# Where the normalised rows wait, and how far the expert weights run ahead, in a two-block kernel on one core

## The chip, the core and the metric

One core of a Trainium2 chip runs the whole program: TensorE (PE, with its weight loads listed as PEld), VectorE (DVE), ScalarE (ACT), GpSimd (POOL) and SyncE (SP), which here only issues DMAs. The metric is the device time of one execution in microseconds. Three runs of the kernel before took 2300.44, 2300.65 and 2302.3 us; the median is 2300.65 us.

## The reference

The program computes two transformer-like blocks on 512 tokens of 1024 channels in float32. The change lies in the last part of the second block, the mixture of experts, and in the last normalisation:

```python
def _rmsnorm(x, g):
    inv = lax.rsqrt(jnp.mean(xf * xf, axis=-1, keepdims=True) + RMS_EPS)
    return xf * inv * g

def _hier_moe(h, wg, bg, we, be, w_gate, w_up, w_down):      # 512 tokens, 64 experts of 1024 x 512
    g_prob = softmax(ht @ wg + bg);  p_g, g_idx = top_k(g_prob, 1)
    e_sel = (ht @ we + be)[group g_idx];  top_l, top_i = top_k(e_sel, 2)
    gate_w = p_g * softmax(top_l);  expert = g_idx * 8 + top_i
    # for every expert, on the rows that chose it:
    a = silu(xb @ w_gate[e]) * (xb @ w_up[e]);  y = a @ w_down[e]
    # each token: sum over its two experts of gate_w * y

x = x + merged @ w_out
hn = _rmsnorm(x, ffn_norm_g)
x = x + _hier_moe(hn, ...)
return _rmsnorm(x, final_norm_g)
```

## The kernel before

All tokens stay in `X` (128 partitions, 4 row blocks i of 1024 columns). The program is written out by hand for each engine, and semaphores alone order the engines among each other. What matters here are three stretches.

**Router.** For each block i, PE multiplies by the output matrix (`project`, L1034), VectorE adds into `X`, ScalarE squares, and the normalising factor `block_r` comes out. PE turns the rows (`turn`, L1045) and makes the router's products (`logits`, L1055). VectorE chooses the experts (`choose`), PE makes a running count of rows of each expert (`rank`, L1071), and VectorE makes from it the table of which token stands in which slot (`place`, `pair_of`). ScalarE writes the normalised rows `Z[:, i, :] = block_r * X` in a turned column order (L1652) and stores them to `hn_d` (L1655), from which the rows of every later pair of experts are gathered. The first pair's rows are not gathered: `first_rows` (L1090) makes them with 64 PE instructions, `Z` as the stationary operand times a selection matrix `OG`. `Z` lies in the first 4096 columns of the work zone.

**Expert pairs.** 64 experts are taken as 32 pairs q, each with room for 64 rows of each expert. A pair needs six matrices of 2 MB: gate, gate, up, up, down, down, numbered n = 6q to 6q+5 (`in_eg`, `in_eu`, `in_ed` in the rows). SyncE loads them in that order (L2920) into a ring of ten slots, `RING`; the slot of matrix n is free again when PE has finished matrix n-10. In the ring's first turn the slots still hold earlier work, so n = 0 waits for the gated products, n = 6 and 7 wait for the output products, n = 8 for the last of these, and n = 9, whose slot is the zone of `Z`, for `hn` 64 (all four blocks stored) and for the first pair's rows. Matrices 10 to 13 are loaded in quarters behind the gate and up products of pair 0 (`refill_first`, L3029); from n = 14 on whole matrices are loaded. PE's pair is: rows turned (L1175), gate and up (L1193, 64 instructions), turn (L1204), down (L1230, 32 instructions). Pairs of odd q are spread onto the tokens by products (`pe_spread`, L1164), the others are stored and gathered. Behind pair 0 PE makes the table of weights (L1139) and the count of rows (`cnt`, L1143), from which the number of further rounds follows.

**End.** Pair 31's down matrices come in three parts (`last0`, `last1`, `last2`), the products (L1218) follow them, eight spread products L1164 and additions L2624 put them onto `X`, ScalarE loads the table of the square root (L1689), squares eight half blocks (L1692), VectorE makes the factor, scales each block (L2710), and SyncE stores it (L3079).

Of the kernel before, what the change touches and what calls it, by code (L numbers as in the profile page):

```python
# [15 lines left out]
CAP = 64  # L16
# [6 lines left out]
SBUF = 55940  # L23
RING = (6, 2, 0, 4, 8, 9, 3, 1, 5, 7)
# [4 lines left out]
def _cols(table, spec):  # L29
    at = 0  # L30
    for name, n in spec:
# [9 lines left out]
CK_N = _cols(CK_COLS, [("ident", 128), ("iota", 128), ("tok", 8), ("gf", 8), ("gx", 8), ("neg", 128), ("cneg", 124), ("c01", 124),  # L41
                       ("tri", 128), ("ones", 128), ("cs", 256)])
# [116 lines left out]
def program(nc, A, out):  # L159
    with ExitStack() as ctx:  # L160
# [202 lines left out]
        done_ck = SB[:, 4096 + CK_COLS["neg"][0]:4096 + CK_N + SM_N + 8 * 72 + 72 + 400]  # L363
# [62 lines left out]
        def tensor_program(pe):  # L426
# [697 lines left out]
            rank(3)  # L1124
            first_rows(2, 1)
# [6 lines left out]

            for q in range(PAIRS):
                pe_pair(pe, T, q, lambda n: loaded("ex", 6 * q + n), lambda n: slot("ex", 6 * q + n), any_bank, ("gather", q % 2, 16 * ((q + 1) // 2)))
                if q == 0:
                    o = open_tile(pe, ("wtab",), any_bank())
                    pe.wait_ge(S("bw"), 1)
                    for n in range(8):
                        ins = pe.matmul(o[:, 0:PAIRS], AM[:, n // 4, n % 4, :], BW[:, n, :], start=n == 0, stop=n == 7)  # L1139
                    ins.then_inc(T.f("wtab"), 1)  # L1140
                    o = open_tile(pe, ("cnt",), any_bank())
                    for j in range(4):
                        ins = pe.matmul(o[:, 0:64], ck("ones"), ES[:, j, :], start=j == 0, stop=j == 3)  # L1143
                    ins.then_inc(T.f("cnt"), 1)
                for n in range(6):
                    W.ended[("ex", 6 * q + n)] = (("g", q), ("g", q), ("u", q), ("u", q), ("d", q, 1), ("d", q, 1))[n]
            pe_spread(pe, PAIRS - 1, LAST_TILES[2:], any_bank)
# [18 lines left out]
        def pe_pair(pe, table, q, ready, weight, bank, gathered):  # L1166
# [12 lines left out]
            for mat, name in enumerate(("g", "u")):  # L1179
# [5 lines left out]
                for k in range(8):  # L1185
# [6 lines left out]
                    for e in range(2):  # L1192
                        ins = pe.matmul(o[64 * e:64 * e + 64, :], x[:, k, 64 * e:64 * e + 64],  # L1193
                                        weight(2 * mat + e)[:, 512 * k:512 * k + 512], start=k == 0, stop=k == 7)
# [14 lines left out]
            if q == PAIRS - 1:  # L1209
                both = [open_tile(pe, ("d", q, nh), bank(), 1, table) for nh in range(2)]  # L1210
                for nh, ks, part in ((0, range(4), 0), (1, range(2), 1), (1, range(2, 4), 2)):
                    if part == 2:
                        pe_spread(pe, q, LAST_TILES[0:2], bank)
                    pe.wait_ge(S(f"last{part}"), 32)
                    for k in ks:
                        for e in range(2):
                            d = 1024 * k + 512 * nh
                            ins = pe.matmul(both[nh][64 * e:64 * e + 64, :], aT[:, k, 64 * e:64 * e + 64], weight(4 + e)[:, d:d + 512],  # L1218
# [6 lines left out]
            for nh in range(2):  # L1225
                o = open_tile(pe, ("d", q, nh), bank(), 1, table)
                for k in range(4):
                    for e in range(2):
                        d = 1024 * k + 512 * nh
                        ins = pe.matmul(o[64 * e:64 * e + 64, :], aT[:, k, 64 * e:64 * e + 64], weight(4 + e)[:, d:d + 512],  # L1230
# [7 lines left out]
        LAST_TILES = [(i, nh) for nh in range(2) for i in range(4)]  # L1238
        BEHIND_X = [(0,), (1,), (2,), (3,), (8,), (9,), (10, 11), (12, 13)]
# [8 lines left out]
        def scalar_program(act):  # L1248
# [388 lines left out]
            for i in range(4):  # L1637
# [17 lines left out]
                act.dma_start(hn_d[128 * i:128 * i + 128, :], Z[:, i, :]).then_inc(S("hn"), 16)  # L1655
# [8 lines left out]
        def act_pair(act, table, q):  # L1664
# [9 lines left out]
            for nh in range(2) if q == PAIRS - 1 else (1,):  # L1674
                act.wait_ge(*table.full("d", q, nh))
# [6 lines left out]
        def results_taken(eng, table, q):  # L1682
            if q - 1 in STORED:
                eng.wait_ge(S("y_st"), 16 * (STORED.index(q - 1) + 1))
            elif q and table is T:
                eng.wait_ge(*table.full("sp", q - 1, 3, 1))

        def act_end(act):
            act.activation(s5, s5, ACT.Sqrt, scale=0.0)  # L1689
            for i, nh in LAST_TILES:  # L1690
                act.wait_ge(S("xadd"), LAST_TILES.index((i, nh)) + 1)
                act.activation(Z[:, i, 512 * nh:512 * nh + 512], X[:, i, 512 * nh:512 * nh + 512], ACT.Square,  # L1692
                               accum_out=h5[:, i, nh:nh + 1]).then_inc(S("l_sq"), 1)
# [6 lines left out]
        def vector_program(dve):  # L1700
# [829 lines left out]
            def place(i):  # L2530
# [6 lines left out]
                for c in range(2):  # L2537
                    t = tt(OC[:, c, :], AM[:, c, i, :], bc(BM0[:, c, i], 1, 128), ALU.mult)
# [20 lines left out]

            def weights():  # L2560
                for i in range(4):
# [21 lines left out]
            def count_rounds():  # L2583
                dve.wait_ge(*T.full("cnt"))
                dve.tensor_reduce(cnt, T.ap("cnt")[:, 0:64], op=ALU.max, axis=AX.X).then_inc(T.s("cnt"), 1)
                dve.wait_ge(*T.free("cnt"))
                after(ts(cnt, cnt, float(CAP - 1), None, ALU.add))
                after(own(dve.tensor_copy(NR, cnt)))
                dve.tensor_scalar(NR, NR, CAP.bit_length() - 1, None, ALU.logical_shift_right).then_inc(S("rounds"), 1)

            for q in range(ENDS):
                dve_pair(dve, T, q, weights if q == 0 else None)
                if q == 0:
                    copy(("wtab",), WTAB, T.ap("wtab")[:, 0:PAIRS])
                    count_rounds()
# [110 lines left out]
        def dve_end(dve):  # L2706
            dve_last(dve, Count(S("last")))
            dve.wait_ge(S("row2"), 16)
            for i in range(4):
                dve.scalar_tensor_tensor(Z[:, i, :], X[:, i, :], r5[:, i:i + 1], row2, ALU.mult, ALU.mult).then_inc(S("fin_row"), 1)  # L2710
# [199 lines left out]
        def sync_program(sp):  # L2910
# [109 lines left out]
            def refill_first(n):  # L3020
                mat = (n - len(RING)) // 2
                for part in range(4):
# [5 lines left out]
                    for e in range(2):  # L3028
                        sp.dma_start(slot("ex", n + e)[:, cols], EW[(n + e) % 6 // 2][2 * ((n + e) // 6) + (n + e) % 2][:, cols]).then_inc(  # L3029
                            loaded("ex", n + e)[0], 16)  # L3030

            for n in range(6 * PAIRS):
# [43 lines left out]
        def sync_end(sp):  # L3076
            for i in range(4):
                sp.wait_ge(S("fin_row"), i + 1)
# [246 lines left out]
```

## Time and profile before

| | us |
|---|---|
| median of three runs | 2300.65 |
| the profiled execution, its own time | 2298.54 |
| its span | 2296.7 |
| PE busy | 2176.2 |
| DVE busy | 936.3 |
| ACT busy | 349.3 |

The page's second part cuts the span into 40 slices of 57 us and shows in each how busy each engine and the 16 DMA engines were. PE is nearly always busy by that view, but its busy share holds for stretches with different limits, so the chain of waits and the rows by stretch say which of PE and the DMA engines sets the pace. The DMA engines moved 563.57 MB, 530.70 MB of it on the queue of SyncE and ScalarE.

### The profile page before, as it was taken

To read this page: it belongs to the slowest core of one execution; us is meant where nothing else is said; L and a number is where in the kernel's file an instruction comes from. 1 tells how busy PE (TensorE), PEld (TensorE's weight loads), DVE (VectorE), ACT (ScalarE), POOL (GpSimd) and SP (SyncE) were. 2 spreads that over 40 slices of the span, in tenths; PEclk is the share of its full clock that TensorE was granted. 3 is DMA by queue.
4 is the path that set the end of the run, shared out by engine and by line. 5 is a ranking of instruction groups with operands and counts; after the bars stand their busy time and mean duration, and the time that the engine had idled before them with its cause. 6 is when DMAs were issued, how large, how long until landed. Compare 5 with 4: busy or idle time off the path is not lost.

```text
span 2296.7 us, 23080 instructions
## 1 busy us (share of the span) xinstructions
PE 2176.2 (95%) x9050; PEld 1131.4 (49%) x9050; DVE 936.3 (41%) x1815; ACT 349.3 (15%) x678; POOL 297.2 (13%) x260
## 2 busy tenths in 40 slices
PE   9999999999999999999999999999999899888886
PEld 6544444475887644477588553333333333333332
DVE  2256544542876587537544342222222222222224
ACT  2015324201222200021101210000000000000001
POOL 0001121221376100001053010000000000000001
PEclk9999999999999999999999999999999999999999
DMA  7211110330333444483332499999999999999997
GB/s 291 101 56 47 55 46 10 115 151 10 110 131 132 160 183 183 172 149 116 128 138 110 201 345 425 427 426 426 426 427 427 426 427 426 426 427 427 427 427 278
DMA packets 75709, 563.57 MB, mean 245 GB/s; under 512 B 21202, under 2 KB 25938, under 8 KB 43152
## 3 DMA queue, kind: packets, MB, share of 16 engines
q1 hardware_dynamic: 52544, 530.70, 57.7%
q10 hardware_dynamic: 15136, 22.71, 3.0%
q0 software_dynamic: 7920, 8.67, 1.1%
q8 instruction: 74, 1.21, 0.2%
q14 instruction: 35, 0.29, 0.0%
HBM read 558.59 MB, written 27.82 MB: 255 GB/s over the span
## 4 chain that ended last, share of the span: by engine, by line
PE 69%; DMA 21%; DVE 6%; SPq 1%; issue 1%; ACT 1%; POOL 0%; DVEq 0%; ACTq 0%; POOLq 0%
DMA sb<-in_eu 13%; PE ps L1193 9%; PE ps L522 9%; PE ps L850 8%; DMA sb<-in_ed 8%; PE ps L429 7%; PE ps L1230 6%; PE ps L771 5%; PE ps L1006 5%; PE ps L454 3%; PE ps L1034 2%; PE ps L732 2%; DVE sb L1704 2%; PE ps L710 2%; PE ps L1164 2%; SPq L3064 1%
## 5 line engine op out<-in xcount | busy, mean ns | idle before, releaser
L1193 PE MATMUL ps<-sb 128*64 128x512 f32 x2048 | 463.0, 607 | 50.9 <-DMA sb<-in_eu 42.4
L1193 PEld LDWEIGHTS ps<-sb 128*64 128x64 f32 x2048 | 163.8, 139 | 337.1 <-issue 337.1
L1704 DVE TENSOR_TENSOR sb<-sb 128x1024 f32<-128x1024 f32 (+9 forms) x419 | 226.4, 573 | 86.3 <-PE ps L850 38.3
L522 PE MATMUL ps<-sb 128*128 128x512 f32 x512 | 236.7, 600 | 0.0
L1230 PE MATMUL ps<-sb 128*64 128x512 f32 x992 | 221.4, 599 | 14.0 <-ACT sb L1672 8.3
L850 PE MATMUL ps<-sb 128*128 128x512 f32 x448 | 193.4, 593 | 1.4 <-DVE sb L2255 1.4
L429 PE MATMUL ps<-sb 128*128 128x512 f32 (+1 forms) x464 | 188.9, 566 | 1.0 <-issue 1.0
L771 PE MATMUL ps<-sb 128*128 128x256 f32 x784 | 175.7, 383 | 3.6 <-DVE sb L2175 3.6
L771 PEld LDWEIGHTS ps<-sb 128*128 128x128 f32 x784 | 148.5, 191 | 25.3 <-DVE sb L2175 4.0
L1230 PEld LDWEIGHTS ps<-sb 128*64 128x64 f32 x992 | 70.6, 137 | 151.9 <-issue 134.9
L522 PEld LDWEIGHTS ps<-sb 128*128 128x128 f32 x512 | 91.0, 190 | 100.3 <-issue 98.6
L850 PEld LDWEIGHTS ps<-sb 128*128 128x128 f32 x448 | 84.6, 190 | 106.7 <-issue 106.7
L429 PEld LDWEIGHTS ps<-sb 128*128 128x128 f32 x464 | 87.6, 190 | 96.1 <-issue 92.7
L1164 PE MATMUL ps<-sb 128*128 128x512 f32 x256 | 119.6, 599 | 0.0
L2696 DVE SCALAR_TENSOR_TENSOR sb<-sb,ps 128x512 f32<-128x512 f32 x32 | 22.1, 690 | 238.3 <-PE ps L1193 238.3
L2691 DVE SCALAR_TENSOR_TENSOR sb<-sb,ps 128x512 f32<-128x512 f32 x32 | 22.1, 690 | 222.5 <-ACT sb L1668 222.5
L1006 PE MATMUL ps<-sb 128*128 128x256 f32 x504 | 109.2, 379 | 1.0 <-issue 1.0
L1006 PEld LDWEIGHTS ps<-sb 128*128 128x128 f32 x504 | 95.7, 190 | 14.7 <-issue 1.8
L1262 ACT ACTIVATE sb<-ps 128x512 f32<-128x512 f32 (+3 forms) x98 | 51.6, 536 | 319.5 <-PE ps L429 54.3
L2624 DVE TENSOR_TENSOR sb<-sb,ps 128x512 f32<-128x512 f32 x128 | 88.0, 688 | 29.8 <-PE ps L1164 29.8
L2742 POOL TENSOR_TENSOR sb<-sb 128x256 f32<-128x256 f32 (+3 forms) x32 | 41.7, 1302 | 351.7 <-DVE sb L1921 351.6
L2686 DVE TENSOR_TENSOR sb<-ps,sb 128x512 f32<-128x512 f32 x64 | 41.4, 688 | 101.3 <-PE ps L1175 100.7
(347 smaller groups left out, 2055.5 us busy)
## 6 DMA issues: line engine op xcount, KB each, us to landing
sb<-in_eu SPq DMA_DIRECT2D x63, 2048.0 KB, 36.7
sb<-in_eg SPq DMA_DIRECT2D x62, 2048.0 KB, 37.3
sb<-in_ed SPq DMA_DIRECT2D x60, 2048.0 KB, 37.3
sb<-in_m SPq DMA_DIRECT2D x16, 2048.0 KB, 7.4
sb<-in_m SPq DMA_DIRECT2D x16, 1024.0 KB, 4.9
sb<-in_mg SPq DMA_DIRECT2D x8, 1536.0 KB, 6.5
sb<-in_wo SPq DMA_DIRECT2D x4, 2048.0 KB, 7.7
sb<-in_winF SPq DMA_DIRECT2D x12, 512.0 KB, 3.5
```

The source lines that it names most:

```text
L429: ins = pe.matmul(out, lhsT, rhs, start=k == 0, stop=k == len(pieces) - 1)
L454: ins = pe.matmul(T.ap(*tile)[:, t], lhsT, rhs[:, t], start=k == 0, stop=k == 7)
L522: ins = pe.matmul(o, lhsT, rhs, start=k == 0, stop=k == 7)
L771: ins = pe.matmul(T.ap(*name)[:, 256 * (f % 2):256 * (f % 2) + 256], a[:, j], b[:, j], start=j == 0, stop=j == 3)
L850: ins = pe.matmul(T.ap("m2", turn, f), a[j], b[j], start=s_ == 0 and j == 0, stop=s_ == 7 and j == 1)
L1006: ins = pe.matmul(o[:, 256 * f:256 * f + 256], a[:, j], b[:, j], start=j == 0, stop=j == n - 1)
L1164: pe.matmul(o, OH[o_ % 2][:, i, :], YE[:, 512 * nh:512 * nh + 512], start=True, stop=True).then_inc(T.f("sp", q, i, nh), 1)
L1193: ins = pe.matmul(o[64 * e:64 * e + 64, :], x[:, k, 64 * e:64 * e + 64], weight(2 * mat + e)[:, 512 * k:512 * k + 512], start=k == 0, stop ...
L1230: ins = pe.matmul(o[64 * e:64 * e + 64, :], aT[:, k, 64 * e:64 * e + 64], weight(4 + e)[:, d:d + 512], start=k == 0, stop=k == 3)
L1262: act.activation(dst, T.ap(*name) if src is None else src, ACT.Copy).then_inc(T.s(*name), 1)
L1704: return own(dve.tensor_tensor(o, a, b, op))
L2624: dve.tensor_tensor(xs, xs, T.ap("sp", q, i, nh), ALU.add).then_inc(S("xadd") if q == PAIRS - 1 else T.s("sp", q, i, nh), 1)
```

## The change

1. **Columns.** In the table of constants, `neg`, `cneg` and `cs` now stand last and 40 columns are added. The constants of finished work give two regions: `HELD`, 1024 columns, for the normalised rows of blocks 0 to 2 one after the other (block 3 takes `YE`), and `FIRST_HALF`, 2048 columns, for half a matrix.
2. **Rows.** ScalarE writes each block's normalised rows to `HELD[i]` and, from block 1 on, first waits until the block before is stored. `first_rows` reads `X` itself, in the order `(a b) -> b a`: its 128 stationary columns now lie 8 floats apart. The factor `block_r` goes into the selection matrix.
3. **Ring.** The zone of `Z` becomes the slot of matrix 6, which waits for the last gated product alone; 7, 8 and 9 take the slots that were those of 6, 7 and 8. The first half of matrix 10 is loaded into `FIRST_HALF` once block 2 is stored and the products `rank` 3 and `cnt` are done.
4. **Count.** The product `cnt` moves from behind pair 0 to behind `rank` 3, its reduction to the start of VectorE's `weights`.
5. **End.** Two spread products go ahead of the product of `last1` and two ahead of that of `last2` (before: two ahead of `last2`). A square root whose result nobody reads stands ahead of ScalarE's copy in pair 31. Block 3 is scaled and stored in two halves.

```diff
-RING = (6, 2, 0, 4, 8, 9, 3, 1, 5, 7)
+RING = (6, 2, 0, 4, 8, 9, 7, 3, 1, 5)
+AHEAD = len(RING)
+        HELD = [view(done_ck, at_ck, 1024)] * 3 + [YE]
+        FIRST_HALF = view(done_ck, 0, 2048)
             def first_rows(i, hf):
-                pe.wait_ge(S("hn_rows"), i + 1)
                 pe.wait_ge(S("first"), i + 1)
-                zr = Z[:, i, :].rearrange("p (b a) -> p b a", b=8)
+                zr = X[:, i, :].rearrange("p (a b) -> p b a", b=8)
...
             rank(3)
+            open_tile(pe, ("cnt",), 4)
+            for j in range(4):
+                ins = pe.matmul(T.ap("cnt")[:, 0:64], ck("ones"), ES[:, j, :], start=j == 0, stop=j == 3)
...
+            def expert(n, at_):
+                return (FIRST_HALF if n == AHEAD and at_ < 2048 else slot("ex", n))[:, at_:at_ + 512]
...
-                    if part == 2:
-                        pe_spread(pe, q, LAST_TILES[0:2], bank)
+                    if part:
+                        pe_spread(pe, q, LAST_TILES[2 * part - 2:2 * part], bank)
...
-                act.activation(Z[:, i, :].rearrange("p (b a) -> p b a", b=8), X[:, i, :].rearrange("p (a b) -> p b a", b=8),
+                if i:
+                    act.wait_ge(S("hn"), 16 * i)
+                act.activation(HELD[i].rearrange("p (b a) -> p b a", b=8), X[:, i, :].rearrange("p (a b) -> p b a", b=8),
                                ACT.Copy, scale=block_r[:, i:i + 1]).then_inc(S("hn_rows"), 1)
...
+                if q == PAIRS - 1 and nh == 0:
+                    act.activation(s5, r5, ACT.Sqrt, scale=0.0)
...
-                    t = tt(OC[:, c, :], AM[:, c, i, :], bc(BM0[:, c, i], 1, 128), ALU.mult)
+                    t = own(dve.scalar_tensor_tensor(OC[:, c, :], AM[:, c, i, :], block_r[:, i:i + 1], bc(BM0[:, c, i], 1, 128),
+                                                     ALU.mult, ALU.mult))
...
+                if n == 6:
+                    sp.wait_ge(*T.full("mgp", 3, 3, 3))
-                if n == 8:
+                if n == 9:
                     sp.wait_ge(*T.full("wo2", 3, 1))
-                if n == 9:
-                    sp.wait_ge(S("hn"), 64)
-                    sp.wait_ge(*T.full("xt", 0, 1))
+                if n == AHEAD:
+                    sp.wait_ge(S("hn"), 48)
+                    sp.wait_ge(*T.full("rank", 3))
+                    sp.wait_ge(*T.full("cnt"))
+                    for part in range(2):
+                        cols = slice(1024 * part, 1024 * part + 1024)
+                        sp.dma_start(FIRST_HALF[:, cols], EW[k // 2][2 * q + k % 2][:, cols]).then_inc(loaded("ex", n)[0], 16)
```

PE's order from the turns of block 3 on, before (a row is a line, an operation and how many in a run; a product counts once here and as two instructions in the trace; L1090 is `first_rows`, L1143 `cnt`, L1193 pair 0's gate and up, L1175 the turns of pair 1):

```order
L1090 MATMUL ps<-sb 128x128 x12
L1071 MATMUL ps<-sb 128x64
L1090 MATMUL ps<-sb 128x128 x4
L1078 MATMUL ps<-sb 128x32 x2
L1090 MATMUL ps<-sb 128x128 x8
L1078 MATMUL ps<-sb 128x32 x2
L1193 MATMUL ps<-sb 64x512 x32
L1204 MATMUL ps<-sb 128x128 x4
L1230 MATMUL ps<-sb 64x512 x16
L1139 MATMUL ps<-sb 128x32 x8
L1143 MATMUL ps<-sb 128x64 x4
L1175 MATMUL ps<-sb 128x128 x8
```

The same place after the change (`first_rows` is L1093, `rank` L1075, `cnt` L1130, gate and up L1199):

```order
L1093 MATMUL ps<-sb 128x128 x12
L1075 MATMUL ps<-sb 128x64
L1130 MATMUL ps<-sb 128x64 x4
L1093 MATMUL ps<-sb 128x128 x4
L1082 MATMUL ps<-sb 128x32 x2
L1093 MATMUL ps<-sb 128x128 x8
L1082 MATMUL ps<-sb 128x32 x2
L1199 MATMUL ps<-sb 64x512 x32
L1210 MATMUL ps<-sb 128x128 x4
L1236 MATMUL ps<-sb 64x512 x16
L1149 MATMUL ps<-sb 128x32 x8
L1181 MATMUL ps<-sb 128x128 x8
```

The four products of the count have left the place between pair 0 and pair 1 and stand ahead of pair 0.

ScalarE's order from its copy in pair 31 to the end, after the change (L1685 is the added square root, L1707 the one of before, L1690 the copies of pair 31's results; the branches are those of the loop of further rounds):

```order
L1681 ACTIVATE sb<-ps 128x512
L1685 ACT_TABLE_LOAD
L1685 ACTIVATE sb<-sb 128x4
L1690 ACTIVATE sb<-ps,sb 128x512 x2
L3170 TENSOR_LOAD sb
...
L3173 UNCONDITIONAL_BRANCH
L1707 ACT_TABLE_LOAD
L1707 ACTIVATE sb<-sb 128x4
L1703 ACTIVATE sb<-sb 128x512 x8
L1711 ACTIVATE sb<-sb 128x4
```

A table load has been added at L1685; the one ahead of the squares still stands, at L1707.

## Rows read from the trace of the kernel before

**Rows 1.** Page, part 2: DMA, tenths of 40 slices.
```profile
DMA  7211110330333444483332499999999999999997
```

**Rows 2.** Chain of waits: start us, us, what.
```profile
1793.80 42.03 DMA sb<-in_eu
```

**Rows 3.** Stretches: length, busy PE, PEld, DVE, ACT, POOL; clock, DMA share, GB/s.
```profile
1300.00:1310.00 10.00, 10.00 (x41) 5.71 (x40) 5.42 (x26) 4.05 (x6) 0.00 (x0) 1.00 0.13 52
...
1344.00:1346.00 2.00, 2.00 (x12) 0.65 (x10) 1.69 (x10) 0.33 (x2) 0.00 (x0) 1.00 0.34 133
...
1480.00:2200.00 720.00, 651.43 (x2818) 248.28 (x2814) 156.99 (x266) 44.90 (x73) 38.22 (x38) 0.98 1.01 426
```

**Rows 4.** Order of time, SyncE's issues: start us, us, what.
```profile
1321.44 0.33 SPq L2920 DMA_DIRECT2D sb<-in_eg  x1
...
1331.79 0.43 SPq L2920 DMA_DIRECT2D sb<-in_eu  x1
...
1346.05 0.33 SPq L2920 DMA_DIRECT2D sb<-in_eu  x1
```

**Rows 5.** Landing (last number) of issues at 1331.42, 1331.79, 1346.05, 1366.31, 1378.00.
```profile
sb<-in_eg SPq DMA_DIRECT2D x1, 2048.0 KB, 7.8
...
sb<-in_eu SPq DMA_DIRECT2D x1, 2048.0 KB, 13.8
...
sb<-in_eu SPq DMA_DIRECT2D x1, 2048.0 KB, 8.2
...
sb<-in_eu SPq DMA_DIRECT2D x1, 2048.0 KB, 15.5
...
sb<-in_ed SPq DMA_DIRECT2D x1, 2048.0 KB, 13.6
```

**Rows 6.** DMA issues of 1372 to 1600, median us to landing.
```profile
sb<-in_ed SPq DMA_DIRECT2D x18, 2048.0 KB, 25.9
```

**Rows 7.** Order of time, PE in the router's end and behind pair 0.
```profile
1335.29 2.90 PE L1090 MATMUL ps<-sb 128*128 128x128 f32 x24
...
1340.55 2.02 PE L1090 MATMUL ps<-sb 128*128 128x128 f32 x16 [0.87 <-DVE sb L2540]
...
1342.87 13.96 PE L1193 MATMUL ps<-sb 128*64 128x512 f32 x64
...
1368.01 1.08 PE L1143 MATMUL ps<-sb 128*128 128x64 f32 x8
```

**Rows 8.** Order of time: weight loads and copies, columns side by side or apart.
```profile
1332.17 0.42 PEld L1045 LDWEIGHTS ps<-sb 128*128 128x128 f32 x4
...
1385.75 0.56 PEld L1204 LDWEIGHTS ps<-sb 128*128 128x128 f32 x4 [1.79 <-issue]
...
1243.83 1.06 ACT L1625 ACTIVATE sb<-sb 128x1024 f32<-128x1024 f32 x1 [9.58 <-DVE sb L1978]
...
1284.86 2.15 ACT L1652 ACTIVATE sb<-sb 128x1024 f32<-128x1024 f32 x1 [1.00 <-DVE sb L2494]
```

**Rows 9.** Order of time, VectorE ahead of pair 1's gate product.
```profile
1370.04 1.29 DVE L2686 TENSOR_TENSOR sb<-ps,sb 128x512 f32<-128x512 f32 x2
```

**Rows 10.** Order of time, the end.
```profile
2271.70 0.69 ACT L1679 ACTIVATE sb<-ps,sb 128x512 f32<-128x512 f32 x1 [5.03 <-PE ps L1218]
...
2273.55 1.94 PE L1218 MATMUL ps<-sb 128*64 128x512 f32 x8 [1.88 <-DMA sb<-in_ed]
...
2275.41 1.99 PE L1164 MATMUL ps<-sb 128*128 128x512 f32 x4
...
2277.33 1.94 PE L1218 MATMUL ps<-sb 128*64 128x512 f32 x8
...
2280.40 1.28 ACT L1689 ACT_TABLE_LOAD   x1 [0.40 <-issue]
```

**Rows 11.** Chain of waits, the squares.
```profile
2281.90 4.92 ACT sb L1692 x16
```

**Rows 12.** Stretches, while blocks are stored.
```profile
2292.00:2293.00 1.00, 0.00 (x0) 0.00 (x0) 1.00 (x2) 0.00 (x0) 0.00 (x0) 0.50 1.00 401
```

More of the change, by code:

```diff
@@ L22 @@
 GELU = math.sqrt(2.0 / math.pi)
-SBUF = 55940
-RING = (6, 2, 0, 4, 8, 9, 3, 1, 5, 7)
+SBUF = 55980
+RING = (6, 2, 0, 4, 8, 9, 7, 3, 1, 5)
+AHEAD = len(RING)
 SM_COLS = {}
@@ L1140, in tensor_program @@
                     ins.then_inc(T.f("wtab"), 1)
[L1141 to L1144, printed above, removed]
                 for n in range(6):
                     W.ended[("ex", 6 * q + n)] = (("g", q), ("g", q), ("u", q), ("u", q), ("d", q, 1), ("d", q, 1))[n]
-            pe_spread(pe, PAIRS - 1, LAST_TILES[2:], any_bank)
+            pe_spread(pe, PAIRS - 1, LAST_TILES[4:], any_bank)
             pe.wait_ge(S("rounds"), 1)
@@ L1193, in pe_pair @@
                         ins = pe.matmul(o[64 * e:64 * e + 64, :], x[:, k, 64 * e:64 * e + 64],
-                                        weight(2 * mat + e)[:, 512 * k:512 * k + 512], start=k == 0, stop=k == 7)
+                                        weight(2 * mat + e, 512 * k), start=k == 0, stop=k == 7)
                     if table is T and q == 0 and k in (1, 3, 5):
@@ L1238, in program @@
         LAST_TILES = [(i, nh) for nh in range(2) for i in range(4)]
+        LAST_ROWS = [(i, slice(0, 1024)) for i in range(3)] + [(3, slice(512 * nh, 512 * nh + 512)) for nh in range(2)]
         BEHIND_X = [(0,), (1,), (2,), (3,), (8,), (9,), (10, 11), (12, 13)]
@@ L2557, in vector_program, with count_rounds @@
             dve_table(dve, own, T)
+            def count_rounds():
+                dve.wait_ge(*T.full("cnt"))
+                dve.tensor_reduce(cnt, T.ap("cnt")[:, 0:64], op=ALU.max, axis=AX.X).then_inc(T.s("cnt"), 1)
+                dve.wait_ge(*T.free("cnt"))
+                after(ts(cnt, cnt, float(CAP - 1), None, ALU.add))
+                after(own(dve.tensor_copy(NR, cnt)))
+                dve.tensor_scalar(NR, NR, CAP.bit_length() - 1, None, ALU.logical_shift_right).then_inc(S("rounds"), 1)
             def weights():
+                count_rounds()
                 for i in range(4):
@@ L2580, in weights @@
                 dve_rows(dve, own, ENDS, EVEN)
[L2583 to L2589, printed above, removed]
             for q in range(ENDS):
@@ L2708, in dve_end @@
             dve.wait_ge(S("row2"), 16)
-            for i in range(4):
-                dve.scalar_tensor_tensor(Z[:, i, :], X[:, i, :], r5[:, i:i + 1], row2, ALU.mult, ALU.mult).then_inc(S("fin_row"), 1)
+            for i, cols in LAST_ROWS:
+                dve.scalar_tensor_tensor(Z[:, i, cols], X[:, i, cols], r5[:, i:i + 1], row2[:, cols], ALU.mult, ALU.mult).then_inc(S("fin_row"), 1)
         def dve_last(dve, own):
@@ L3028, in refill_first @@
                     for e in range(2):
+                        if n + e == AHEAD and part < 2:
+                            continue
                         sp.dma_start(slot("ex", n + e)[:, cols], EW[(n + e) % 6 // 2][2 * ((n + e) // 6) + (n + e) % 2][:, cols]).then_inc(
@@ L3076, in sync_end @@
         def sync_end(sp):
-            for i in range(4):
-                sp.wait_ge(S("fin_row"), i + 1)
-                sp.dma_start(out[128 * i:128 * i + 128, :], Z[:, i, :]).then_inc(S("fin"), 16)
-            sp.wait_ge(S("fin"), 64)
+            for n, (i, cols) in enumerate(LAST_ROWS):
+                sp.wait_ge(S("fin_row"), n + 1)
+                sp.dma_start(out[128 * i:128 * i + 128, cols], Z[:, i, cols]).then_inc(S("fin"), 16)
+            sp.wait_ge(S("fin"), 80)
         R_more, R_pair = (Psum(PS, T.s_full, T.s_free) for _ in range(2))
```

29 lines of the change are left out of this document (17 added, 12 removed).

## The prediction

> **What bounds the kernel now.** I read the page's second part first, then the chain of waits, then the table of stretches and the landing times of SyncE's loads.
>
> The DMA row of the page is at 9 in every slice from about 1310 us on, and has holes only before [rows 1]. In the chain of waits of the late pairs the long pieces are transfers, such as 42.03 us of an up matrix [rows 2], and from 1480 to 2200 us the DMA share is 1.01 at 426 GB/s while PE is busy 651 of 720 us [rows 3]. So from pair 5 or so the end of the program is: the moment from which the DMA engines never rest, and the bytes still to be moved. Nothing in the change takes bytes away. It can help only by moving bytes into the holes, which are in the router's stretch: share 0.13 in 1300 to 1310 us, and 0.34 in 1344 to 1346 us [rows 3], and the last hole decides.
>
> How near the DMA engines are to a hole at any later time is told by the landings. A 2 MB load that finds the engines idle lands after 7.8 us (8.2 for another) [rows 5]. What a load takes over that is work queued ahead of it. Matrix 14, issued at 1366.31 when PE frees its slot, takes 15.5: 7.7 us are queued ahead. Matrix 16, issued at 1378.00 behind pair 1's gate product, takes 13.6: only 5.8 us. By 1372 to 1600 the median of the down matrices is 25.9 [rows 6]; PE gets through a pair faster there than the engines bring one, so the queue grows.
>
> **Part 1, the ring: what is gained before PE comes in.** Matrix 6 goes out behind matrix 5 at some 1266 us, into the hole. Of the old issues at 1321.44, 1331.79 and 1346.05 [rows 4] the last goes: matrix 9 now takes the place of matrix 8 and lands where that landed, 1331.79 + 13.8 = 1345.6, not at 1346.05 + 8.2 = 1354.2. That is 8.6 us of lead: one matrix (4.9 us at 426 GB/s) and the hole in which matrix 9 waited for the last rows to be stored. The half of matrix 10 (2.5 us), sent when the count is done at about 1339, keeps the engines busy until the first quarters are free, so the lead isn't lost at once.
>
> **Part 2: how much of the lead survives.** The following slots are freed by PE, and PE is no faster. Matrix 14 can't be led by more than the 7.7 us queued ahead of it, matrix 16 by no more than 5.8, plus what PE gains up to there. PE gains the count: four products (0.92 us until the turns can begin) from 1368.01 [rows 7], and VectorE's copy of the turned rows, which stood behind the count's reduction and began at 1370.04 [rows 9]. With the count away the first half of the rows is turned at about 1368.01 + 0.42 + 0.2 and copied from 1368.7: 1.35 us sooner. So the bound at matrix 16 is 5.8 + 1.35 = 7.15 us, the smallest of the three. Later ones have larger queues and the same 1.35 us. If PE's start of pair 0 slips by d, all these bounds shrink by d: the gain is 7.15 - d.
>
> **Part 3: d, what it costs PE.** The 64 instructions of `first_rows` stand in PE's row with no gap but one of 0.87 us [rows 7]: 24 take 2.90 us with the tail of the last, 0.112 us each. Their weight loads now read columns 8 floats apart. No row shows a weight load so. The nearest on PE are the turns at L1204, 4 floats apart: four loads in 0.56 us against 0.42 for columns side by side [rows 8], 0.035 us more each; the other near row is on ScalarE, where the copy of 1024 columns 8 floats apart takes 2.15 us and a tanh of 1024 side by side 1.06 [rows 8], a factor of 2.03. Bounds: nothing (the load is hidden under the product), 64 x 0.035 = 2.2 us by the first, 64 x 0.112 x 1.03 = 7.4 us by the second; beyond it a load could cost what ScalarE's element costs in time, 2.15/1024 x 128 = 0.27 us, 64 x 0.16 = 10 us. The product itself takes about as long as the load, so a doubled load has nothing to hide under. I take the factor of distance 8, a little rounded down for overlap: 6.5 us.
>
> The Trainium skill, SBUF — State Buffer, section "Door 1: The DMA port swizzle", says that the memory is read in lines of 16 bytes and that float32 may be read up to 4 elements apart for free, with a penalty beyond. The trace agrees as far as it goes: 4 apart costs PE little, 8 apart doubles ScalarE's time. The page gives no size; by it the free case is out, by the loads 4 apart alone it would be likely.
>
> The rest of the router: the count's four products (0.9 us) stand where PE waits 0.87 us for VectorE's L2540 [rows 7], so they cost nothing while the loads are cheap, and if the loads are dear that wait is gone and the count adds what the wait gave. The factor in the selection matrix replaces two operations of 128x128 by two of the same form: 0. The wait for `hn_rows` never ended last. ScalarE's new waits for its stores: each store has more than 9 us before the next copy needs it: 0. VectorE's reduction of the count (0.9 us) delays pair 0's gate step, which has the up product beside it (7 us of the 13.96 [rows 7]): 0. Pair 0 starts 6.5 us late, at 1349.4.
>
> Sum for the DMA stretch: -7.15 + 6.5 = -0.65 us.
>
> **Part 4, the end.** Before, PE's row is: `last1` lands, product at 2273.55, two spreads at 2275.41, `last2` lands, product at 2277.33 [rows 10]. ScalarE's copy, begun at 2271.70 and 0.69 long, lets spreads start at 2272.4. With two spreads there (1.8 us) the `last1` product starts at 2274.2, not 2273.55; then two more spreads, and the `last2` product at 2277.9, not 2277.33: +0.55. The spreads it takes forward don't matter, since the squares follow from ScalarE's last copy on: table load 1.28 us [rows 10], then eight squares back to back, 4.92 us [rows 11]. The order of instructions shows the table load of the end still in its place, and a second one added in pair 31 where ScalarE waits 5.03 us for a product [rows 10]: 0, no gain. Were the load gone, VectorE's additions would end last and 1.4 us would be had.
>
> The halved last block: while blocks are stored the DMA share is 1.00 at 401 GB/s [rows 12], so the stores follow the engines and not VectorE. A smaller last piece saves at most the 0.6 us that half a block takes to move; the extra operation costs 0.1. I take -0.1.
>
> **Sum.** -0.65 + 0.55 - 0.1 = -0.2 us against the profiled execution's 2298.54 (span 2296.7 and 1.84 around it). The runs' median is 2.1 us above that; against it the same difference gives 2300.4 us.
>
> **The rivals.** What can be told from no change here is about 0.2%, 4.6 us.
> - *The stride is hidden or nearly free on PE (d from 0 to 2).* For it: the loads 4 apart cost only 0.035 us, and loads are pulled ahead of products. Against: the factor 2 at distance 8 on ScalarE. Gain 5.2 to 7.15, end +0.45: 2294 to 2296, faster.
> - *Partly hidden (d from 2 to 5).* 2296 to 2299, within the band.
> - *The strided loads cost more than ScalarE's rate* (two readings of float32 per product both going line by line, and VectorE's chain waiting behind PE's `rank` 3, L1071). Place: the 64 loads before pair 0. It decides from d = 7.15 + 4.15 = 11.3 us, 0.29 us a load. At 0.33 us: d = 14, 2300.65 - 7.15 + 14 + 0.45 = 2308. For it only that no row shows distance 8 on PE. Slower.
> - *The lead isn't made*, because block 2's store lands late and holds the half matrix: then 1 us or so less in the free case, nothing in mine, where matrix 16 bounds.
>
> **Chances.** Forecast, load about doubled (d from 5 to 9, 2298.5 to 2302.5): 0.53. Free or nearly: 0.26. Partly hidden: 0.14. Dearer: 0.07. The range over all but two in ten, from the free case's lower end to a load somewhat above ScalarE's rate: 2293.8 to 2303.5. Faster by over 0.2% is the free case less its upper edge, 0.25; slower the dear one, 0.06; within, 0.69.
>
> **What would show it.** The group of weight loads of `first_rows`: near 0.21 to 0.23 us apart, and pair 0's first gate product near 1349. At 0.12 apart and 1343 the first rival holds. Matrix 9 should land at about 1345.6; matrix 16 should land 7.8 to 8 us after its issue, with a dip of the DMA share just before. The end from `last1` on should be half a microsecond longer, with a table load of 1.28 us still before the squares. I am wrong altogether if matrix 16's load takes much more than 8 us to land although the time doesn't fall, or if the DMA share has holes after 1400 us.

## The result, and the profile after

The changed kernel takes 2307.74 us (median of 9 runs, 2306.1 to 2309.61), the kernel before 2300.65 on the same chip: a ratio of 1.0031, 95% interval 1.0023 to 1.0040. It is slower, by 7.1 us, and lies outside the range. The profiled execution took 2306.10 us, 7.6 more than that of before, and its span is 7.3 us longer.

The page's DMA row reads like the one of before [rows 1]; averages over 58 us do not show what changed. The last row is the rate.

```profile
span 2304.0 us, 23083 instructions
...
DMA  7211110330333444483333589999999999999996
GB/s 290 100 55 47 55 46 10 113 152 10 110 131 132 164 178 182 183 152 116 113 137 114 237 308 422 425 425 426 426 425 426 426 425 426 426 426 426 426 426 267
```

PE in the router's end, in order of time (start, length, instructions). These are the lines of [rows 7]; L1093 is `first_rows`.

```profile
1333.16 1.94 PE L1093 MATMUL ps<-sb 128*128 128x128 f32 x8
...
1335.38 2.08 PE L1093 MATMUL ps<-sb 128*128 128x128 f32 x8
...
1339.02 5.97 PE L1093 MATMUL ps<-sb 128*128 128x128 f32 x24
1344.83 0.33 PE L1075 MATMUL ps<-sb 128*128 128x64 f32 x2
1345.00 1.06 PE L1130 MATMUL ps<-sb 128*128 128x64 f32 x8
1345.89 2.12 PE L1093 MATMUL ps<-sb 128*128 128x128 f32 x8
...
1348.21 4.08 PE L1093 MATMUL ps<-sb 128*128 128x128 f32 x16
1352.59 3.65 PE L1199 MATMUL ps<-sb 128*64 128x512 f32 x16
```

The 24 instructions that took 2.90 us take 5.97: 5.81/24 = 0.242 us each against 0.114. Over 64 that is 8.2 us; the difference of the five groups is 8.0. Pair 0's first gate product starts at 1352.59 instead of 1342.87 [rows 7], 9.7 us late. Of that 1.9 were lost before `first_rows`: this execution ran at half clock for 6.8 us from 92 us on, that of before for 3.4, which makes 1.7 of it. VectorE now waits for `rank` 3, which stands behind the 24 on PE:

```profile
1345.27 0.29 DVE L1720 TENSOR_TENSOR sb<-sb,ps 128x128 f32<-128x128 f32 x1 [3.60 <-PE ps L1075]
```

Behind pair 0, again PE:

```profile
1379.34 13.95 PE L1199 MATMUL ps<-sb 128*64 128x512 f32 x64 [0.54 <-DVE sb L2703]
...
1395.65 8.79 PE L1236 MATMUL ps<-sb 128*64 128x512 f32 x32 [0.69 <-ACT sb L1681]
```

Pair 1 starts 26.75 us after pair 0. Before it was 28.01 (1370.88 for its start), so the count's removal gave 1.3 us.

The DMA engines in the stretch where the last hole of before lay [rows 3]; the last two numbers are share and GB/s:

```profile
1345.00:1350.00 5.00, 5.00 (x30) 5.00 (x29) 2.79 (x11) 0.00 (x0) 0.00 (x0) 1.00 0.85 286
1350.00:1352.00 2.00, 2.00 (x10) 2.00 (x9) 0.69 (x1) 0.00 (x0) 0.00 (x0) 1.00 0.39 158
1352.00:1354.00 2.00, 2.00 (x14) 1.10 (x15) 1.53 (x8) 0.00 (x0) 0.00 (x0) 1.00 0.00 0
1354.00:1356.00 2.00, 2.00 (x12) 0.65 (x10) 1.76 (x14) 0.33 (x2) 1.40 (x2) 1.00 0.23 47
1356.00:1360.00 4.00, 4.00 (x22) 1.36 (x20) 3.38 (x17) 0.28 (x1) 0.81 (x1) 1.00 0.94 271
1360.00:1364.00 4.00, 4.00 (x22) 1.37 (x20) 0.69 (x1) 0.32 (x1) 0.00 (x0) 1.00 0.91 283
...
1480.00:2200.00 720.00, 652.65 (x2848) 251.52 (x2848) 159.53 (x269) 45.06 (x74) 38.56 (x38) 0.99 1.01 426
```

SyncE's issues, by which this reads: matrices 8 and 9 at 1333.36 and 1333.73 (landed at 1341.6 and 1347.9), the half matrix at 1346.14 (landed at 1352.05), the first quarter only at 1354.57, when pair 0 has used the first quarter of a slot, matrix 16 at 1386.46. So the engines stand idle for 2.5 us ahead of the first quarter. The quarters of matrices 10 to 13 are the first transfers that PE releases, and PE is late.

```profile
1333.36 0.80 SPq L2937 DMA_DIRECT2D sb<-in_eu  x2
1346.14 1.00 SPq L3069 DMA_DIRECT2D sb<-in_ed  x2
1354.57 6.29 SPq L3048 DMA_DIRECT2D sb<-in_ed  x6
...
1386.46 0.80 SPq L2937 DMA_DIRECT2D sb<-in_ed  x2
```

Landing of the matrix issued at 1386.46 (last number), against 13.6 in [rows 5]: nothing is queued ahead of it.

```profile
sb<-in_ed SPq DMA_DIRECT2D x1, 2048.0 KB, 8.8
```

Most of the lead is gone before matrix 16, though. Against before, this execution has moved 1.87 MB more by 1350 us, 1.04 MB less by 1364 and 1.65 less by 1400. Matrix 16 is issued 8.5 us later than before and lands 3.7 later (1395.3 against 1391.6); by matrix 24 the lag is 5.3, and the first half of the last up matrix lands at 2262.5 instead of 2257.2, 5.3 late. The rest arises at the end [rows 10]:

```profile
2274.33 1.28 ACT L1685 ACT_TABLE_LOAD   x1
2274.36 3.65 PE L1224 MATMUL ps<-sb 128*64 128x512 f32 x16 [0.69 <-ACT sb L1681]
...
2278.85 1.96 PE L1170 MATMUL ps<-sb 128*128 128x512 f32 x4 [0.83 <-issue]
2280.74 1.94 PE L1224 MATMUL ps<-sb 128*64 128x512 f32 x8
2282.61 1.98 PE L1170 MATMUL ps<-sb 128*128 128x512 f32 x4
2284.52 1.94 PE L1224 MATMUL ps<-sb 128*64 128x512 f32 x8
2286.51 0.69 ACT L1690 ACTIVATE sb<-ps,sb 128x512 f32<-128x512 f32 x1 [7.75 <-PE ps L1224]
...
2287.59 1.28 ACT L1707 ACT_TABLE_LOAD   x1 [0.39 <-issue]
```

The product of `last0` starts 6.35 us later than before (2274.36 against 2268.01), 1.05 more than the transfers' lag: PE's last pair waits for no transfer here, since the clock fell twice shortly before (share and clock at 2204 to 2212 below). From that product to ScalarE's last copy it is 12.15 us instead of 11.30, all of it work of PE but for 0.83 in which the first spread waits for ScalarE's copy: +0.85. From that copy to the end it is 17.5 us in both. 5.3 + 1.05 + 0.85 = 7.2.

The clock (the third number from the end, 0.5 is 1.2 GHz, 1 is 2.4) in three short stretches of the same execution:

```profile
94.00:98.00 4.00, 4.00 (x16) 2.07 (x13) 0.00 (x0) 0.00 (x0) 0.00 (x0) 0.50 0.05 16
...
1395.00:1400.00 5.00, 4.35 (x14) 1.35 (x16) 0.00 (x0) 0.59 (x1) 0.00 (x0) 0.66 1.01 429
...
2204.00:2212.00 8.00, 6.17 (x16) 2.09 (x18) 0.27 (x1) 0.00 (x0) 0.00 (x0) 0.57 1.00 418
```

Every profile here has such drops, 3.4 or 6.8 us long; each 3.4 us cost PE 1.7 (pair 1's 32 down products took 8.79 us at 1395.65, 7.09 at the full clock). Before these three PE had waited: 3.44 us, 0.94 and 0.69 around the turn L1210, and 2.92 us for an up matrix. The one at 1396 cost no transfer time, since the DMA engines were full (share 1.01).

### The profile page after: what moved, and what is told of

The parts are those of the page before. It is cut to its first block, busy times and chain, and to the rows that moved or that the text cites. A ratio compares the mean times of both kernels' runs of the same rounds, so it can differ in the third digit from the quotient of the medians.

```text
span 2304.0 us, 23083 instructions
## 1 busy us (share of the span) xinstructions
PE 2186.5 (95%) x9050; PEld 1140.8 (50%) x9050; DVE 936.8 (41%) x1816; ACT 350.6 (15%) x680; POOL 297.9 (13%) x260
## 4 chain that ended last, share of the span: by engine, by line
PE 72%; DMA 18%; DVE 7%; ACT 1%; issue 1%; ACTq 1%; SPq 0%; POOL 0%; DVEq 0%; POOLq 0%
DMA sb<-in_ed 12%; PE ps L1199 11%; PE ps L526 9%; PE ps L854 8%; PE ps L1236 7%; PE ps L433 6%; DMA sb<-in_eu 5%; PE ps L775 5%; PE ps L1010 5%; PE ps L1170 3%; PE ps L458 3%; PE ps L1038 2%; PE ps L736 2%; DVE sb L1720 2%; PE ps L714 2%
## 5 line engine op out<-in xcount | busy, mean ns | idle before, releaser
L1199 PE MATMUL ps<-sb 128*64 128x512 f32 x2048 | 458.4, 603 | 44.4 <-DMA sb<-in_eu 36.2
L1199 PEld LDWEIGHTS ps<-sb 128*64 128x64 f32 x2048 | 162.3, 139 | 327.5 <-issue 327.4
L1720 DVE TENSOR_TENSOR sb<-sb 128x1024 f32<-128x1024 f32 (+8 forms) x411 | 224.7, 579 | 86.1 <-PE ps L854 38.3
```

Source lines behind the costliest of these rows:

```text
L1720: return own(dve.tensor_tensor(o, a, b, op))
```

## The experiments

The runs come in three groups, named a_ and b_, p_, and c_, each on a chip of its own with its own runs of the kernel before (2300.22, 2300.41 and 2299.79 us, over 30 runs each). A median of about ten runs is good to some 2 us (the intervals), so differences of 1 us between two of them are weak alone. The same kernel under two names shows it: 2297.84 us as p_spread and 2296.26 as c_spread.

**The new ring with cheap loads (a_plain).** Pair 0's rows are read side by side from `X`, and the first four matrices are loaded with their rows in the same order; the factor of the norm follows.

```diff
-                zr = X[:, i, :].rearrange("p (a b) -> p b a", b=8)
+                zr = X[:, i, :].rearrange("p (b a) -> p b a", b=8)
...
-                                  bc(ck("gx")[:, 4 * hf:4 * hf + 4], 2, 128), ALU.mult).then_inc(table.s("xt", q, hf), 1)
+                                  bc(ck("gf" if table is T and q == 0 else "gx")[:, 4 * hf:4 * hf + 4], 2, 128), ALU.mult).then_inc(table.s("xt", q, hf), 1)
...
+                    if n < 4:
...
+                        sp.dma_start(shaped(slot("ex", n), 8, 512),
+                                     A[("eg", "eu")[k // 2]][k % 2].rearrange("(t p) n -> p t n", p=P)).then_inc(loaded("ex", n)[0], 16)
+                        continue
```

> The changed kernel, but the first pair's stationary columns of X lie side by side again: its gate and up matrices are loaded with row 128 t + p on partition p, so that the turned rows may be taken as contiguous blocks of 128. Nothing is left out of the computation. Theory 1 (the loads 8 apart cost PE about 8 us before pair 0, and PE frees the slots that bound the DMA engines): load spacing back from 0.24 to 0.11 us, pair 0's gate product 8 us sooner than in the changed kernel, the time 6 to 8 us below the changed kernel's and 0 to 1% of nothing else: about 2295 to 2300 where before gives 2300.65. Theory 2 (the loads cost little at the end, the loss is in the end or in the constants' new places): the time falls by less than 2 us against the changed kernel, to 2306 or more.

Measured 2296.74 us, ratio 0.9989 (0.9980 to 0.9998): within 2295 to 2300, and 11.0 us below the changed kernel (on another chip), more than the 6 to 8 expected. The loads are back at 0.114 us and pair 0 starts at 1343.29:

```profile
1335.66 2.90 PE L1093 MATMUL ps<-sb 128*128 128x128 f32 x24
...
1343.29 13.95 PE L1199 MATMUL ps<-sb 128*64 128x512 f32 x64
```

The rest of the change makes the kernel faster; the column order alone turns its sign. But the first half of the last up matrix lands at 2252.6, 4.6 us sooner than before, not 7. Matrix 9 and the half matrix do bring the lead: by 1350 us 2.92 MB more have moved than before (6.8 us at 426 GB/s). By 1360 it is 2.58, by 1390 2.20, by 1500 2.15 (5.0 us). The first part goes here:

```profile
1350.00:1352.00 2.00, 2.00 (x12) 0.65 (x10) 1.43 (x5) 0.60 (x1) 0.47 (x1) 1.00 0.94 262
1352.00:1354.00 2.00, 2.00 (x12) 0.64 (x10) 0.00 (x0) 0.00 (x0) 0.00 (x0) 1.00 0.93 258
```

The share is over 0.9 and the rate 260, against 408 and 363 in the same two stretches before: the queue is nearly empty and holds quarters and small stores and gathers. Matrix 14 lands 6.9 us sooner than before and matrix 16 only 5.45: it is issued 0.84 sooner (1377.16), and takes 9.0 us to land with nothing queued ahead of it, not 7.8.

A second part goes where the engines are full. From 1500 to 2200 us the two profiles with the old ring (before, b_apart) move 298.50 and 298.54 MB, the twelve with the new ring 297.94 to 298.06. These 0.5 MB are 1.1 us at the same DMA share of 1.01. The prediction has no term for them, and what in the new ring makes the rate lower stays open.

**The same with the end of before (a_plain_oldend), and the change with the end of before (a_oldend).** The edit on top of each:

```diff
-                if q == PAIRS - 1 and nh == 0:
-                    act.activation(s5, r5, ACT.Sqrt, scale=0.0)
...
-                    if part:
-                        pe_spread(pe, q, LAST_TILES[2 * part - 2:2 * part], bank)
+                    if part == 2:
+                        pe_spread(pe, q, LAST_TILES[0:2], bank)
...
-LAST_ROWS = [(i, slice(0, 1024)) for i in range(3)] + [(3, slice(512 * nh, 512 * nh + 512)) for nh in range(2)]
+LAST_ROWS = [(i, slice(0, 1024)) for i in range(4)]
```

> The same, with the end as before: spread products in the old order, no added square root, the last block scaled and stored whole. Theory 1 with my term for the end (0.45 us lost): 0.3 to 0.7 us below the run with the new end. Theory 2 (the end costs several us): 2 us or more below it.

> The changed kernel with the end as before. Theory 1: 2307.2, half a microsecond below the changed kernel, and the columns 8 apart keep the rest. Theory 2 (the end is the loss): 2304 or less.

Measured 2295.40 us, ratio 0.9981 (0.9972 to 0.9990), and 2305.28, ratio 1.0024 (1.0014 to 1.0034). The first is the best version found; it beats both kernels. It lies 1.3 us below a_plain and the second 2.5 below the changed kernel (another chip): each between what the two theories say, so the end costs more than 0.45 us. On one chip: the new end costs 1.3 us (2296.74 - 2295.40), the strided loads 9.9 (2305.28 - 2295.40), the new ring and count with cheap loads give 4.8.

**The strided loads with the old ring (b_apart).** The kernel before, with `X` read 8 apart and the factor in the selection matrix.

```diff
-                pe.wait_ge(S("hn_rows"), i + 1)
...
-                zr = Z[:, i, :].rearrange("p (b a) -> p b a", b=8)
+                zr = X[:, i, :].rearrange("p (a b) -> p b a", b=8)
...
-                    t = tt(OC[:, c, :], AM[:, c, i, :], bc(BM0[:, c, i], 1, 128), ALU.mult)
+                    t = own(dve.scalar_tensor_tensor(OC[:, c, :], AM[:, c, i, :], block_r[:, i:i + 1], bc(BM0[:, c, i], 1, 128),
+                                                     ALU.mult, ALU.mult))
```

> The kernel before, with one thing of the change: the first pair's products read X with columns 8 apart, the factor goes into the selection matrix. Theory 1 by the queue of 5.8 us ahead of matrix 16: pair 0 starts 8 us late, 5.8 us of it are covered, the time rises by about 2 us, to 2303. If all of the 8 us reach the end: 2308.5. Theory 2 (no loss from the loads): 2300.7.

Measured 2303.68 us, ratio 1.0015 (1.0006 to 1.0023): +3.5 us. The same loads cost the same on PE:

```profile
1338.81 5.92 PE L1089 MATMUL ps<-sb 128*128 128x128 f32 x24
```

From the start of `first_rows` to pair 0 it is 18.5 us instead of 11.6: the 8 us less most of the 0.87 us wait at L2540. Half of these 6.9 us reach the end. The forecast of about 2303 came close by luck, for the queue ahead of matrix 16 does not decide it: that matrix still lands 10.4 us after its issue, so some work is still queued ahead. The time is lost sooner, in front of matrix 9, the second of these two:

```profile
1333.54 18.06 SPq L2920 DMA_DIRECT2D sb<-in_eu  x2
```

```profile
1350.00:1352.00 2.00, 2.00 (x14) 1.67 (x15) 0.79 (x3) 0.00 (x0) 0.00 (x0) 1.00 0.00 0
```

Matrix 9 waits for the stores of the normalised rows and for `first_rows`. Before, the stores ended last, at 1346.04, and `first_rows` had been done since 1342.6: 3.5 us of slack. In b_apart the stores land at 1347.93 and `first_rows` ends at 1351.19, 3.3 us behind them; matrix 9 goes out at 1351.27. From 1360 to 2200 us the lag in bytes stays between 2.1 and 2.4 MB (5.0 to 5.6 us, 1.7 of it from the router, where this execution had one clock drop more). With the new ring matrix 9 no longer waits for `first_rows`, but there PE's own release of the first quarters comes last, and the whole price arrives at the end, 9.9 us. The strided load and the new ring are each tolerable alone and not together.

**Is it the delay, or something else about strided reading? (p_work)** a_plain_oldend with a product of 152 columns behind each of the 32 of `first_rows`; the results of these products are never read.

```diff
+                    extra = pe.matmul(PS[:, 1024:1024 + 152], zr[:, k, :], X[:, i, 0:152], start=True, stop=True)
```

> The version with columns side by side and the old end (2295.4 where before gave 2300.2), with 32 further products of 128x152 put among the first pair's rows; their results are overwritten and never read. Their two passes take about 0.25 us each, 8 us in all, as much as the loads 8 apart cost. Theory 1 (only PE's delay before pair 0 counts): the time of the changed kernel with the old end, 5 us above before, so about 2305. Theory 2 (the strided loads do something more, for instance the drop of the granted clock to 0.5 for 3.4 us near 1370 to 1396 that each profile with such loads shows and none without): no such drop, and the time 1.5 to 2 us lower, about 2303.5.

Measured 2304.24 us, ratio 1.0019 (1.0010 to 1.0028). Pair 0 starts at 1351.13, 7.65 us after a_plain_oldend's, and the time is 8.8 above it (on another chip). From the start of `first_rows` to pair 0 it is 8.0 us longer, in a_oldend 7.7. The time lies midway between the two theories' 2305 and 2303.5 and does not decide between them; what speaks is the size, 8.8 us for 8.0: nearly all that the strided loads cost comes with a plain delay of PE at this place. It also has a clock drop behind pair 0 (clock 0.72 in 1366 to 1372), with columns side by side, and p_nohalf_cnt below, with cheap loads and no delay, has one between 1362 and 1368, so those drops do not need strided reading.

**The half matrix and the count (p_nohalf, p_nohalf_cnt).** a_plain_oldend with matrix 10 all in quarters in its own slot, and that with the count behind pair 0 again.

```diff
-                        if n + e == AHEAD and part < 2:
-                            continue
...
-                if n == AHEAD:
...
-                return (FIRST_HALF if n == AHEAD and at_ < 2048 else slot("ex", n))[:, at_:at_ + 512]
+                return slot("ex", n)[:, at_:at_ + 512]
```

```diff
-            open_tile(pe, ("cnt",), 4)
-            for j in range(4):
-                ins = pe.matmul(T.ap("cnt")[:, 0:64], ck("ones"), ES[:, j, :], start=j == 0, stop=j == 3)
-            ins.then_inc(T.f("cnt"), 1)
...
+                    o = open_tile(pe, ("cnt",), any_bank())
+                    for j in range(4):
+                        ins = pe.matmul(o[:, 0:64], ck("ones"), ES[:, j, :], start=j == 0, stop=j == 3)
+                    ins.then_inc(T.f("cnt"), 1)
...
-                count_rounds()
...
+                    count_rounds()
```

> The version with columns side by side and the old end, without the half matrix: all of matrix 10 comes into its ring slot in quarters. My bound (matrix 16 limits the lead to 7.15 us whatever runs ahead): about 0.5 us slower than with the half, 2296. If what is moved ahead counts in full: 1 MB is 2.5 us, 2298.

> The same without the half, and with the count and its reduction behind pair 0 again, as before. By my step (the count holds up pair 1 by 1.35 us, and matrix 16 is bound by that): 1.0 to 1.4 us slower than without the half alone. If the lead is lost elsewhere: the same time.

Measured 2296.46 us, ratio 0.9982 (0.9973 to 0.9991), and 2297.68, ratio 0.9985 (0.9976 to 0.9994). The count's place gives 1.2 us, as large as the shift seen in PE's rows, but the runs of the two scatter by 6 and 8 us, so the medians alone do not show it. p_nohalf comes out as the bound at matrix 16 had it (2296, against 2298 if all that is moved ahead counted); the half matrix was run again below.

**The end in parts (p_spread, c_spread, c_store) and the half matrix again (c_nohalf), over one base (c_oldend).** c_oldend is a_plain_oldend; p_spread and c_spread are that with the new spread order alone, c_store with the halved store alone, c_nohalf is p_nohalf. Their edits are parts of those above.

> The version with columns side by side, with the new order of the spread products alone (old store, no added square root). By my term: 0.55 us slower than with the old order (2295.4 against before's 2300.2). By the two profiles of the end (PE stands 0.84 us before the first spread, then is 1.9 us late): 1.0 to 1.4 us slower, and then nothing is left for the halved store and the square root, since the run with all three is 1.3 us slower.

> The new ring and count with block-ordered columns (X read side by side for pair 0) and the end of before: the common base of these four, 2295.4 in the first call. By both theories 2295 to 2296.5. The other three are read against it on this chip.

> The base plus the new spread order alone. Theory S (products of last1 and last2 queue behind spreads that wait for ScalarE's copy): 1.0 us over the base. Theory N (the 2.4 us seen across two calls is all of it clock drops and chips): within 0.3 us of the base. A difference of 2 us or more would say that the order costs more than the row of PE shows.

> The base plus the halved store of the last block alone. The distance from ScalarE's last copy to the end was 17.4 to 17.5 us with and without it: by that, no difference (within 0.3 us). The rival of the prediction's term: 0.1 us less.

> The base without the half matrix held apart (matrix 10 all in quarters). If the half matrix carries lead over the thin stretch: 1 us over the base; if the lead is bounded by PE's slots alone, as the prediction had it: no difference (within 0.3 us).

| | us | ratio and interval |
|---|---|---|
| p_spread (its own group) | 2297.84 | 0.9992 (0.9983 to 1.0001) |
| c_oldend | 2295.59 | 0.9985 (0.9976 to 0.9994) |
| c_spread | 2296.26 | 0.9989 (0.9980 to 0.9998) |
| c_store | 2295.61 | 0.9983 (0.9974 to 0.9992) |
| c_nohalf | 2296.80 | 0.9989 (0.9980 to 0.9998) |

On one chip the medians put the spread order at 0.7 us, the halved store at 0.0, and leaving the half matrix out at 1.2. The 0.7 lies between theories S and N and settles neither. Of p_spread's 2.4 us over a_plain_oldend only 0.2 is in the kernel before of the two chips, and 1.6 went when the same kernel ran as c_spread: scatter, for the most part. The half matrix shows in the rate just before and while pair 0 starts: c_nohalf, then c_oldend:

```profile
1344.00:1350.00 6.00, 6.00 (x36) 2.82 (x36) 5.25 (x27) 0.32 (x2) 0.61 (x1) 1.00 0.77 251
```

```profile
1344.00:1350.00 6.00, 6.00 (x35) 2.80 (x36) 5.25 (x27) 0.32 (x2) 0.26 (x1) 1.00 0.98 386
```

But the lead does not last. c_oldend has moved 0.86 MB more by 1350 us (171.30 against 170.44), and by 1400 both stand at 191.1, with pair 0 begun at the same time (1345.06 and 1345.09); p_spread and p_nohalf, 0.70 MB apart at 1350, also agree by 1400. So the traces show the half matrix to gain nothing that reaches the end, and the 1.2 us between the medians, inside their intervals, is not shown to be its work.

Spread order, c_oldend, PE: a wait of 1.77 us for a transfer ahead of `last1`'s product (what ended the 1.92 before `last0`'s the trace doesn't name), and 11.2 us from `last0`'s product to ScalarE's last copy.

```profile
2265.43 3.65 PE L1224 MATMUL ps<-sb 128*64 128x512 f32 x16 [1.92 <-issue]
...
2270.86 1.94 PE L1224 MATMUL ps<-sb 128*64 128x512 f32 x8 [1.77 <-DMA sb<-in_ed]
2272.72 1.98 PE L1170 MATMUL ps<-sb 128*128 128x512 f32 x4
2274.64 1.94 PE L1224 MATMUL ps<-sb 128*64 128x512 f32 x8
2276.51 5.42 PE L1170 MATMUL ps<-sb 128*128 128x512 f32 x12
2276.62 0.69 ACT L1688 ACTIVATE sb<-ps,sb 128x512 f32<-128x512 f32 x1 [6.81 <-PE ps L1224]
```

c_spread: no wait for a transfer is left, but the chain on PE is 12.1 us long.

```profile
2261.26 3.65 PE L1224 MATMUL ps<-sb 128*64 128x512 f32 x16 [1.38 <-ACT sb L1681]
...
2265.75 1.96 PE L1170 MATMUL ps<-sb 128*128 128x512 f32 x4 [0.83 <-issue]
2267.63 1.94 PE L1224 MATMUL ps<-sb 128*64 128x512 f32 x8
2269.50 1.99 PE L1170 MATMUL ps<-sb 128*128 128x512 f32 x4
2271.41 1.94 PE L1224 MATMUL ps<-sb 128*64 128x512 f32 x8
2273.40 0.69 ACT L1688 ACTIVATE sb<-ps,sb 128x512 f32<-128x512 f32 x1 [7.75 <-PE ps L1224]
```

Squares can't start before ScalarE's last copy, so a spread put ahead of the last products does not shorten anything; it only moves them back.

## Why the prediction was wrong

The forecast was 2300.4 us, the measured time is 2307.74. The kind of mechanism held: a late PE eats the lead of the DMA engines one for one. Two terms of the sum failed: d, the price of the strided loads (6.5 us, where PE shows 8.0 and the runs 9.9), and the lead that survives (7.15 us, where the runs show 4.2 to 4.8). In us, with the differences of medians on one chip:

| term | predicted | runs | from |
|---|---|---|---|
| lead of the new ring and count | -7.15 | -4.8, -4.2 | a_plain_oldend and c_oldend against before |
| strided loads | +6.5 | +9.9 | a_oldend - a_plain_oldend |
| the end | +0.45 | +1.3, +0.7 | a_plain - a_plain_oldend; c_spread and c_store over c_oldend |
| sum | -0.2 | +6.4, or +6.4 | measured +7.1 |

(The two sums take the first or the second value of the first and third rows, -4.8 + 9.9 + 1.3 and -4.2 + 9.9 + 0.7.)

- **Part 1, the lead is made: right.** Matrix 9 lands at 1347.9, and at 1346.0 without the 1.9 us by which this router ran late; 1345.6 was worked out. a_plain is 6.8 us ahead by 1350.
- **Part 2, what survives: mis-sized, by 2.4 to 3 us.** "Can't be led by more than the 5.8 us queued ahead of it, plus 1.35" takes a lone load to land in 7.8 us. Matrix 16 does land with nothing ahead of it, but in 9.0 us (a_plain), so it lands 5.45 us sooner than before and not 7.15. Then 1.1 us more goes in the long full stretch, where the new ring moves 0.5 MB less. The part also leaves out the quarters of matrices 10 to 13, which PE releases ahead of matrix 14: the first took 9.6 us to land before and 4.0 with the engines idle (the changed kernel), so 5.6 us were queued ahead of it, less than ahead of matrix 16 with the count's gain. The 1.35 for the count was right (1.3 in PE's rows).
- **Part 3, d: the step that failed first.** "I take the factor of distance 8, a little rounded down for overlap: 6.5 us." There is no overlap to round down for: a load costs 0.242 us, 2.1 times the old one, and the 64 cost 8.0 to 8.2. That is just above the bound of 7.4 got from ScalarE's factor, and inside the outer bound of 10. The comparison of time per column would have been better than that of factors: 0.242/128 = 1.9 ns, ScalarE's 2.15/1024 = 2.1 ns [rows 8]. The row of loads 4 apart, which fed the rival that the stride is free, says nothing of loads 8 apart: the step between 4 and 8 is abrupt. By the Trainium skill, SBUF — State Buffer, section "Door 1: The DMA port swizzle", float32 up to 4 elements apart is free and beyond it is penalised; the traces agree in kind, though 4 apart is not quite free (0.035 us a load for 4, 0.13 for 8).
- **From d to the time.** The prediction had the time follow d one for one once the queue is empty. It does, and rather more: 9.9 us for 8.0 to 8.2, and 8.8 for p_work's 8.0 across chips. The profiles point to the clock for the excess. In a_oldend it fell from 1369.6 to 1373.0 us, just ahead of the release of matrices 14 and 16, and from 1370 to 1400 us that execution moved 11.20 MB, the changed kernel's, whose drop came at 1396, 12.11: 2.1 us. p_work's fell at 1368.1. These are single executions, so how much of the excess of the medians is clock stays open.
- **The point of decision was set wrong.** I put the slower case at d = 11.3. With the lead at 4.5, the end at 1.0 and the 4.6 us of the band it lies at 4.5 + 4.6 - 1.0 = 8.1 us, which the loads just reach. Both errors had to meet (even together they give 2300.65 - 4.5 + 8.0 + 1.0 = 2305.2; the rest is the excess above): with d at 8.0 and the lead as predicted the time would have been 2302.0, and with d at 6.5 and the measured lead 2303.1.
- **The rest of the router: right.** The count costs PE 0.9 us ahead of pair 0 and gives 1.3 behind it; the wait for `hn_rows` and the selection matrix show nothing in PE's row.
- **The half matrix: as the prediction had it, by the traces.** The fourth rival gave it nothing under this case, since matrix 16 bounds, and its 0.86 MB of lead at 1350 us are gone by 1400 (c_oldend against c_nohalf). The medians differ by 1.2 us, within their intervals.
- **Part 4: right in kind.** The table load of 1.28 us is still there at L1707. The halved store gives 0.0 instead of -0.1. The order of spreads costs 0.85 to 0.95 in PE's rows (0.7 between two medians) instead of 0.55: I held the transfers' landings fixed but counted only the spreads' own length, not that the first waits 0.83 us for ScalarE's copy with the `last1` product behind it.

## What to carry to other kernels

Look whether a product's stationary operand is read at a stride before moving it: at 8 floats apart a weight load took twice its time, more than the product beside it could hide, and reordering the other operand's rows in the load from memory removed it for nothing here. A delay is free only as far as something else ends later: with the old ring matrix 9 waited for stores, and 3.5 of 6.9 us were hidden there. When an edit takes such slack away, every later delay of the engine that frees the buffers counts in full; so price two such edits together (b_apart +3.5, the lead -4.8, both +5.1). Bytes moved by a given time, compared between two kernels, show where a lead is lost and whether it lasts. And a DMA share near 1 is no sign of full rate: read GB/s beside it when the queue is short.

## What the runs showed of the hardware

- Weight loads of 128 float32 columns 8 apart follow each other at 0.242 us against 0.114 side by side; ScalarE's copy at the same distance (2.15 us) takes twice what a tanh of as many columns side by side does (1.06).
- The granted clock falls to 1.2 GHz for 3.4 or 6.8 us while PE works (in the three drops shown, soon after waits of 0.7 to 3.4 us), at places that differ between executions of the same program, and costs PE 1.7 us per 3.4. It makes profiles of one kernel differ by more than some edits are worth: two identical kernels, a_plain_oldend and c_oldend, started pair 0 at 1343.48 and 1345.06, the second with one drop more, at 642 us.
- 16 engines at a share of 0.93 moved 258 GB/s with quarters and small transfers queued, and 426 with 2 MB matrices.
- The twelve profiles with the new ring moved 297.94 to 298.06 MB from 1500 to 2200 us, the two with the old ring 298.50 and 298.54, all at a DMA share of 1.01.
